# A hybrid attention/RWKV-7/MoE decoder layer: two projection loops with 512-column products, and the wo weight halves split in other places

## What is computed

```
h = RMSNorm(x); z = h @ w_in                       # 2048 -> 5944 columns
y_a = RMSNorm(sparse attention(z))                 # 8 heads, 1024 wide
y_b = RWKV-7 time mixing(z)                        # 16 heads, 1024 wide
x += concat(y_a, y_b) @ w_out                      # 2048 x 2048
x += (softmax(q k^T) v) @ wo                       # q = RMSNorm(x) @ wq; k, v from 256 memory tokens; 4 heads of 512
x += HierMoE(RMSNorm(x))                           # one of 4 groups, 2 of its 8 experts
out = RMSNorm(x)
```

## Time and profile before

| | us |
|---|---|
| median of 3 runs (lowest, highest) | 1764.54 (1761.72, 1767.03) |
| the profiled execution's own time | 1765.84 |
| its span | 1764.1 |
| PE busy | 1687.6 |
| DVE busy | 1011.5 |
| ACT busy | 760.9 |
| mean granted TensorE clock | 0.986 |

### The profile page before, as it was taken

One profiled execution on the slowest core, in us unless ns is written; L12 is line 12 of the kernel. 1 busy time (PEld: TensorE's weight loads), 2 busy tenths in 40 slices (PEclk: granted clock), 3 DMA queues, 4 the chain that ended last, 5 costly groups with the idle time before them and its releaser, 6 DMA issues.

```text
span 1764.1 us, 29546 instructions
## 1 busy us (share of the span) xinstructions
PE 1687.6 (96%) x12488; PEld 1468.0 (83%) x12488; DVE 1011.5 (57%) x1260; ACT 760.9 (43%) x964; POOL 71.6 (4%) x136
## 2 busy tenths in 40 slices
PE   7999999999999999999999999989999999999996
PEld 5887887878878889999999989967887887888784
DVE  1142533424434554445454334388889889889986
ACT  1011210111114544444343333446776766777674
POOL 4001010101100000000000000000000000000000
PEclk9899999999999999999999999999999999999999
DMA  7430613306126444445535326239998996999993
GB/s 211 143 96 2 198 50 123 123 2 198 50 77 213 151 137 144 136 152 192 190 120 182 127 75 195 112 137 356 376 376 328 380 375 249 372 375 349 357 375 150
DMA packets 173745, 350.77 MB, mean 199 GB/s; under 512 B 12915, under 2 KB 145612, under 8 KB 148172
## 3 DMA queue, kind: packets, MB, share of 16 engines
q1 hardware_dynamic: 173644, 349.30, 56.0%
HBM read 347.18 MB, written 2.10 MB: 198 GB/s over the span
## 4 chain that ended last, share of the span: by engine, by line
PE 85%; DVE 10%; ACT 2%; POOL 1%; issue 1%; DMA 1%; SPq 0%; DVEq 0%; ACTq 0%
PE bank L1288 17%; PE bank L771 16%; PE bank L1133 10%; PE bank L1307 9%; PE bank L1137 5%; PE bank L1029 4%; PE bank L1036 3%; DVE split L2172 3%; PE bank L790 2%; PE bank L760 2%; DVE piece L1993 1%; PE bank L876 1%; PE bank L891 1%; PE bank L886 1%; DVE arena_phases L2276 1%; PE bank L1183 1%
## 5 line engine op out<-in xcount | busy, mean ns | idle before, releaser
L2172 DVE TENSOR_TENSOR split<-weights_raw,split 128x2048 fp32r<-128x2048 f32 x192 | 438.7, 2291 | 53.9 <-ACT split L1711 50.7
L1711 ACT CAST split<-weights_raw 128x2048 fp32r<-128x2048 f32 x192 | 367.2, 1914 | 94.5 <-PE bank L1288 48.3
L1288 PE MATMUL bank<-split,gathered_hi 128*128 128x512 f32 x1024 | 320.6, 394 | 7.0 <-DVE split L2172 6.9
L771 PE MATMUL bank<-arena_fixed 128*128 128x256 f32 x1280 | 302.6, 388 | 0.0
L771 PEld LDWEIGHTS bank<-arena_fixed 128*128 128x128 f32 x1280 | 238.5, 191 | 42.8 <-issue 9.1
L1288 PEld LDWEIGHTS bank<-split,gathered_hi 128*128 128x128 f32 x1024 | 190.2, 189 | 48.1 <-DVE split L2172 9.5
L1288 PE MATMUL bank<-split,gathered_lo 128*128 128x512 f32 x512 | 200.7, 392 | 0.0
L1133 PE MATMUL bank<-loop_split,act_over_concat 128*128 128x256 f32 x768 | 164.8, 283 | 0.0
L1307 PE MATMUL bank<-split,hidden_hi 128*128 128x512 f32 x512 | 161.1, 395 | 1.5 <-DVE hidden_lo L2314 1.0
L2076 DVE TENSOR_TENSOR loop_split<-arena_fixed,loop_split 128x2048 fp32r<-128x2048 f32 x48 | 107.8, 2289 | 90.8 <-ACT loop_split L1608 90.8
L1133 PEld LDWEIGHTS bank<-loop_split,act_over_concat 128*128 128x128 f32 x768 | 129.1, 192 | 0.1
(11 more groups left out here) (396 smaller groups left out, 2388.8 us busy)
## 6 DMA issues: line engine op xcount, KB each, us to landing
weights_raw<-in_moe_w_gate_dram SPq DMA_DIRECT2D x64, 1024.0 KB, 5.0
weights_raw<-in_moe_w_up_dram SPq DMA_DIRECT2D x64, 1024.0 KB, 7.0
weights_raw<-in_moe_w_down_dram SPq DMA_DIRECT2D x32, 2048.0 KB, 7.6
arena_fixed<-in_w_in_dram SPq DMA_DIRECT2D x22, 2048.0 KB, 8.9
arena_fixed<-in_wv_mem_dram SPq DMA_DIRECT2D x8, 2048.0 KB, 8.5
arena_fixed<-in_w_out_dram SPq DMA_DIRECT2D x8, 2048.0 KB, 8.1
arena_fixed<-in_wq_mem_dram SPq DMA_DIRECT2D x8, 2048.0 KB, 8.1
arena_fixed<-in_wo_mem_dram SPq DMA_DIRECT2D x8, 2048.0 KB, 8.3
```

Source lines behind the costliest of these rows:

```text
L771: mm = pe.matmul(b[:, half * T:half * T + T], w[:, c, half * P:half * P + P], hT[:, c, :], start=st, stop=en)
L1288: mm = pe.matmul(bank[parity][:, :], hs[a][:, group % 2, NC // 4 * off + c, :], sl[:, b, c * 2 * FF:(c + 1) * 2 * FF], start=off + c + k == 0,
L1711: nc.scalar.copy(split_half(i, 0, j), raw_half(j, hf, tail)).then_inc(act_hi, 1)
L2172: V.tensor_tensor(split_half(i, 1, j), raw_half(j, hf, tail), split_half(i, 0, j).bitcast(F32), ALU.subtract).then_inc(dve_lo, 1)
```

## The change

It has four parts.

1. For n = 0 and 2 a step takes 512 columns (`WC`) at once. The two slots of a step hold two halves of the rows (8 chunks x 512 columns each) in place of two halves of the columns. A `loop_split` tile is now 4 chunks x 512 columns. PE (`looped_tokens`) does for it 2 token halves x 4 chunks x 3 passes = 24 products of 512 columns, into whole banks, and the pairs of banks alternate from step to step. Row chunks 8 to 15 come first for w_out, in slot 0, so the attention outputs are needed from the third tile on; for wo the outputs of heads 2 and 3 are needed from the third tile on.
2. The residual is added once per step and token half, 128x512; the first token half's add waits for a new semaphore `pe_first`, which PE raises after the last product of that token half, 12 products before the step's end. The squares are 128x512, one per token half, each after its own add, and on ACT they follow the casts. The sums have 4 parts per token half (`SUMMED`).
3. For n = 0 and 2 the loops of PE, DVE and SP are written out, not hardware loops; ACT keeps its loops.
4. The casts and subtractions of wo's second tile pair are moved. ACT: after the copies of heads 2's and 3's probabilities, one half there and one between the output casts of heads 2 and 3. DVE: one half before the lo part of head 2, one between those of heads 2 and 3.

The wq loop keeps its code as `looped_turned`. The core of the diff:

```diff
+        def loop_source(wv_, n, i, s):
+            if n == 1:
+                return wv_[:, :, bass.ds((2 * i + s) * UC, UC)]
+            k = NC // 2 * (s ^ (n == 0))
+            return wv_[:, k:k + NC // 2, bass.ds((2 * i) * UC, WC)]
...
+                if n != 1:
+                    for i in range(1, PAIRS):
+                        for s in range(2):
+                            load_looped(i, s)
+                    continue
...
+            def looped_tokens(n, src, src_ready, turn=0):
+                for q in range(PAIRS):
+                    pe.wait_ge(out_loop, n * NLU + max(2, 2 * q))
+                    for s in range(2):
+                        for h in range(2):
+                            pe.wait_ge(loop_lo, 4 * q + 2 * (NLU * n + s) + h + 1)
+                            pe.wait_ge(src_lo, src_ready[s])
+                            for half in range(2):
+                                b = bank[2 * (q % 2) + half][:, :]
+                                for c in range(NC // 4):
+                                    cc = NC // 2 * (s ^ turn) + NC // 4 * h + c
+                                    for k, (x_, y_) in enumerate(PASSES):
+                                        end = s + h == 2 and c == NC // 4 - 1 and k == 2
+                                        mm = pe.matmul(b, src(x_, cc)[:, half * P:half * P + P],
+                                                       lspl[2 * s + h][:, y_, c * WC:c * WC + WC],
+                                                       start=s + h + c + k == 0, stop=end)
+                                if s + h == 2 and half == 0:
+                                    mm.then_inc(pe_first, 1)
+                        mm.then_inc(pe_loop, 1)
...
-            looped(2, True, normed, (SRC_MEM + MH // 2, SRC_MEM + MH))
+            looped_tokens(2, normed, (SRC_MEM + MH // 2, SRC_MEM + MH))
...
+            def squares(i, n):
                 for tt in range(NT):
+                    act.wait_ge(out_loop, n * NLU + tt + 3 + 2 * i)
+                    A(square_junk[:, tt, bass.ds(i * WC, WC)], x[:, tt, bass.ds(i * WC, WC)], ACT.Square,
+                      accum_out=rms_p[:, tt, bass.ds(i, 1)]).then_inc(squared, 1)
...
-                    if h == 1:
-                        loop_weights(2 * NLU, 1)
+                    if h == MH - 2:
+                        loop_half(1, 1)
+                if (what, h) == ("t", MH - 1):
+                    act.wait_ge(loop_full[1], 16 * NLU + 16)
+                    loop_half(1, 0)
...
+                    if residual and s == 1:
                         for tt in range(NT):
+                            if tt == 0:
+                                dve.wait_ge(pe_first, i + PAIRS * (n // 2) + 1)
+                            else:
+                                dve.wait_ge(pe_loop, 2 * i + n * NLU + 2)
+                            xs = x[:, tt, bass.ds(i * WC, WC)]
+                            V.tensor_tensor(xs, xs, bank[2 * (i % 2) + tt][:, :], ALU.add).then_inc(out_loop, 1)
...
-            loop_weights(2 * NLU, 1)
+            loop_half(2 * NLU, 1, 0)
             output_lo(MH - 2)
+            loop_half(2 * NLU, 1, 1)
             output_lo(MH - 1)
```

More of the change, by code:

```diff
@@ L685, in _ @@
                     sp.dma_start(rb[:, NGR:], router_expert_b[0].partition_broadcast(P)).then_inc(s_late, 16)
-                with sp.Fori(int(n != 1), NLU // 2) as i:
+                if n != 1:
[3 more added lines that the diff above has]
+                    continue
+                with sp.Fori(0, NLU // 2) as i:
                     for s in range(2):
@@ L1128, in looped @@
                                 for c in range(NC // 2):
-                                    cc = NC // 2 * (h ^ turn) + c
                                     for k, (x_, y_) in enumerate(PASSES):
[L1131 to L1138, removed]
+                                        at = c * UC + half * P
+                                        mm = pe.matmul(b, lspl[2 * s + h][:, y_, at:at + P], src(x_, NC // 2 * h + c),
+                                                       start=h + c + k == 0, stop=h == 1 and c == NC // 2 - 1 and k == 2)
                         mm.then_inc(pe_loop, 1)
@@ L1605, in _, with loop_half, loop_weights @@
                     gap2()
[L1606 to L1610, removed]
+            def loop_half(s, h):
+                nc.scalar.copy(lspl[2 * s + h][:, 0, :], slot(s)[:, h * HU:h * HU + HU]).then_inc(loop_hi, 1)
+            def loop_weights(at, s):
                 act.wait_ge(loop_full[s], 8 * at + 16)
                 for h in range(2):
-                    loop_half(s, h, turn)
-            def squares(i, s, n):
-                act.wait_ge(out_loop, n * NLU + s + 3 + 2 * i)
+                    loop_half(s, h)
+            def squares(i, n):
                 for tt in range(NT):
-                    A(square_junk[:, tt, bass.ds((2 * i + s) * UC, UC)], x[:, tt, bass.ds((2 * i + s) * UC, UC)], ACT.Square,
-                      accum_out=rms_p[:, tt, bass.ds(2 * i + s, 1)]).then_inc(squared, 1)
+                    act.wait_ge(out_loop, n * NLU + tt + 3 + 2 * i)
+                    A(square_junk[:, tt, bass.ds(i * WC, WC)], x[:, tt, bass.ds(i * WC, WC)], ACT.Square,
+                      accum_out=rms_p[:, tt, bass.ds(i, 1)]).then_inc(squared, 1)
             def loop_stream(n, out_copy=False, last=False):
                 def step(i, s, weights):
-                    if out_copy:
+                    if out_copy or weights:
                         act.wait_ge(pe_loop, 2 * i + n * NLU + s + 1)
-                    else:
-                        squares(i, s, n)
                     if out_copy:
@@ L1635, in step @@
                     if weights:
-                        loop_weights(2 * i + n * NLU + 2, s, turn)
-                turn = int(n == 0)
+                        loop_weights(2 * i + n * NLU + 2, s)
+                    if not out_copy and s == 1:
+                        squares(i, n)
                 with act.Fori(0, NLU // 2 - 1) as i:
@@ L1652, in _ @@
                 normed_hi("na", f, c_nsa, lambda c: over_hT[:, c, :]).then_inc(src_hi, 1)
-            loop_half(0, 1, 1)
-            loop_weights(0, 1, 1)
+            loop_half(0, 1)
+            loop_weights(0, 1)
             loop_stream(0)
@@ L1819, in rms @@
                     dve.wait_ge(squared, SUMMED[name])
-                    link(V.tensor_reduce(rms_s, rms_p[:, :, 0:4] if name == "nf" else rms_p, AX.X, ALU.add))
+                    link(V.tensor_reduce(rms_s, rms_p if name == "na" else rms_p[:, :, 0:4], AX.X, ALU.add))
                 else:
@@ L2089, in _ @@
                 normed_lo(f, c_nsa, lambda c: over_concat[:, c, :], lambda c: over_hT[:, c, :]).then_inc(src_lo, 1)
-            loop_half(0, 0, 1, 1)
-            loop_weights(0, 1, 1)
+            loop_half(0, 0, 1)
+            loop_weights(0, 1)
             def loop_stream(n, residual=True, last=False):
                 def step(i, s, weights):
-                    if residual:
-                        dve.wait_ge(pe_loop, 2 * i + n * NLU + s + 1)
+                    if residual and s == 1:
                         for tt in range(NT):
-                            xs = x[:, tt, bass.ds((2 * i + s) * UC, UC)]
-                            ins = V.tensor_tensor(xs, xs, bank[2 * s + tt][:, 0:UC], ALU.add)
-                        ins.then_inc(out_loop, 1)
-                    if weights:
-                        loop_weights(2 * i + n * NLU + 2, s, turn)
-                turn = int(n == 0)
+                            if tt == 0:
[4 more added lines that the diff above has]
+                            V.tensor_tensor(xs, xs, bank[2 * (i % 2) + tt][:, :], ALU.add).then_inc(out_loop, 1)
+                    if weights:
+                        loop_weights(2 * i + n * NLU + 2, s)
+                if residual:
+                    for i in range(PAIRS):
+                        for s in range(2):
+                            step(i, s, i < PAIRS - 1 or (s == 0 and not last))
+                    return
                 with dve.Fori(0, NLU // 2 - 1) as i:
```

31 lines of the change are left out of this document (17 added, 14 removed).

## The result

The changed kernel took 1750.16 us (median of 4 runs, 1748.86 to 1752.25) against 1765.63 us (median of 4, 1761.72 to 1767.03) for the one before. The ratio is 0.9917 with a 95% interval of 0.9898 to 0.9937: 14.7 us less, between 11.1 and 18.0. (The medians themselves lie 15.5 us apart.) At a line of 2%, 35 us, it counts as the same; at the 0.3% of the prediction it is faster. A later comparison with 5 runs gave 0.9899 (0.9882 to 0.9915), 1749.69 against 1767.35 us. The forecast was 1748.0 us, 0.9906 of the 1764.54 us that it started from, with a range of 1743.5 to 1755.5.

A forecast was written before the change was run, and what follows sets the result against it. PE was taken as the bound, busy 1687.6 of 1764.1 us. Terms of 9.9, 6.1 and 0.5 us sum to 16.5, giving 1748.0 us from the median of 1764.5; range 1743.5 to 1755.5 us.

The forecast's parts named there:

- rival d: Loops' ends: the clock holds there too, up to 3.2 us more at one loop, 1744.8 us; chance 0.12.
- Term 1: w_out and wo loops: 384 products of 512 columns at 226.7 ns each replace 768 at 120.0; 9.9 us less.
- The wait at the start of w_out: Start of w_out: PE still waits for DVE's tile 1, so the first tile's 0.3 us gain becomes a wait.
- Term 2: Memory heads: head 2's values start 3.5 us sooner and the clock holds, 2.6 us more; 6.1 us less.
- Term 3: Ends of both loops: sums start some 1.5 us after the last product, not 1.75; 0.5 us less for both.
- (a): Heads: clock falls before head 2's values anyway, or DVE or ACT hold them longer; gain 3.5 us, 1750.6 us; chance 0.08.
- (b): Both loops: 512-column products cost 232.9 ns as at L1307; gain 5.5 in place of 10.2 us, 1752.7 us; chance 0.12.
- (c): Both loops: 512-column products cost 240 ns, so widening gains nothing; 1757.9 us; chance 0.03.
- (e): Both loops: fetching written-out code makes PE wait, up to 49 us, time 1797; chance 0.03.
- The third unit of wo: wo loop: this tightest load is in time, needed 21.8 us after the start, with 2.6 us of slack; costs nothing.

The follow-up runs named there:

- gap filled: Kernel before, with 17 unused products on PE after the memory heads' last transposes: 1763.09 us, ratio 0.9978.
- written out: Kernel before, with only PE's loops over w_out and wo written out in place of the hardware loop: ratio 1.0004.
- part 4 alone: Kernel before, with only wo's second tile pair's casts and subtractions moved behind the probability copies: 1758.97 us, ratio 0.996.
- other banks: Changed kernel, with head 2's outputs in PSUM banks 2 and 3 and head 3's in 5 and 6: 1748.52 us, ratio 0.9901.
- changed, again: The changed kernel itself, unaltered, measured again in a later comparison with the kernel before: 1749.69 us, ratio 0.9899.
- all but part 4: Changed kernel, with wo's weight casts put back before the probability copies: 1755.3 us, ratio 0.9938.
- alternate banks: Changed kernel, with the wide products changing PSUM bank after every three, not every twelve: 1750.39 us, ratio 0.9905.
- late adds: Changed kernel, with both token halves' adds waiting for the end of the step: 1750.73 us, ratio 0.9909.
- busy ends: Changed kernel, with 11 idle products on PE at the end of the w_out and wo loops: 1746.74 us, ratio 0.9885.
- busy ends, other banks: Changed kernel, with idle products at both loops' ends and swapped PSUM banks for heads 2 and 3's outputs: 1746.33 us, ratio 0.9882.

## Why the prediction was right, and where it was not

The sum was 16.5 us, and the profiled span is shorter by 15.6 us (1764.1 to 1748.5). Step by step:

| step | forecast | measured in the chain |
|---|---|---|
| w_out loop | -4.8 | -4.7 (first product to last: 807.45 to 900.12, 809.17 to 897.13) |
| wo loop | -5.1 | -5.1 |
| heads | -6.1 | -5.4 |
| sums after the loops | -0.5 | -0.5 |
| clock behind the loops' ends | 0 (rival d: up to -3.2 at one) | -1.3 and -1.5 |
| before the w_out loop | 0 | +1.7 |
| after the norm before the MoE | 0 | +1.2 |

The total lies so near the forecast partly by luck. The three costed terms gave 15.7 us in place of 16.5; the clock behind the loops' ends, put at nothing, gave 2.8 more, and 2.9 were lost in two places that the change does not touch. Those two are scatter between executions. The first product of w_out stands at 807.45, 808.04, 811.10 and 811.37 us in the profiles of four kernels whose code up to there is the same (before, gap filled, written out, part 4 alone). From the MoE's first gate product to the end, the twelve profiles take 592.9 to 594.5 us; from the last product of wo to that gate product, the 32 transposing instructions left out, those four kernels take 28.6 to 29.8 us.

**Term 1** held to a tenth: 226.8 against 226.7 ns. The wait at the start of w_out came as costed:

```profile
815.17 0.30 PEld L1149 LDWEIGHTS bank<-loop_split,rwkv_outputs_hi 128*128 128x128 f32 x2 [0.71 <-DVE loop_split L2108]
```

The weight load waits 0.71 us for tile 1, where it waited 0.22 before. The reason I gave for 226.7 rather than 232.9 ns (the bank change) fell with the experiment. So the choice of L1288's price was right, but its reason was not, and what does set the two prices apart is not shown. L1288's own groups of 24 do not all cost 226.7 ns either: 21 of the 55 in the chain of before do, 27 cost 228.8 to 229.2. At 229 ns each loop would have gained 0.9 us less. The Trainium skill's figure (TensorE: Matmul & The Clock Gate, "Wait — 56ns, not 53.3ns?") of about 2.5 ns beside the columns does not fit products that each carry a weight load: here it was 13.3 to 13.5 ns, and merging two saved 13.2.

**Term 2** is the one that was off: 6.1 forecast, 5.4 measured. The mechanism was right in both its halves: the clock gave 2.7 us (2.6 forecast), and the shorter wait 2.7 (3.5 forecast). The step that failed is "PE's values of head 2 start 3.5 us sooner, at about 1030.1, after 0.9 us of idle time". I had checked ACT's order and not all of PE's waits at that instruction. `memory_values` also waits for DVE's lo part of head 1, since head 2's outputs go into head 1's banks. Under the 4.4 us of before that wait had been over for 2.8 us when PE started and had no row of its own. Its end was in the trace of before all the same:

```profile
1029.49 1.29 DVE L2126 TENSOR_TENSOR act_over_hT<-bank,act_over_concat 128x512 fp32r<-128x512 f32 x2 [2.76 <-ACT act_over_concat L1678]
```

It ends at 1029.49 + 1.29 = 1030.8, 0.7 us behind my start. The run with other banks took this wait away, and the idle time fell to 0.78 us.

**Term 3** came out at 1.5 us from last product to sum (897.1 to 898.62), as summed:

```profile
898.62 0.16 DVE L1852 TENSOR_REDUCE arena_fixed<-arena_fixed 128x2 f32<-128x8 f32 x1 [0.79 <-ACT square_junk L1651]
```

**Rivals.** (a) came true in part: the clock held behind 1.70 us, but DVE did hold head 2's values, by 0.8 of the 2.6 us that (a) put at stake. (b) and (c) are out by the chain, (e) by the written-out kernel. (d) was half seen. I had treated the clock there as decided by the length of the idle time, and it is not. The clock fell at both ends in the changed kernel's profile, at a cost 1.3 and 1.5 us lower than before; in its second profile it did not fall at all behind the wo loop. The row of before for that place:

```profile
1138.85 6.73 PE L790 MATMUL bank<-norm_diagonals,arena_phases 128*128 128x128 f32 x32 [3.22 <-DVE norm_diagonals L1831]
```

The 1.5 us there can't be credited to the change: the kernel with part 4 alone has the old loop and the same 3.22 us of idle, and its 32 instructions take 5.47 us. (d)'s price was also too high: at the full rate the 64 transposing instructions take 7.81 us, not 7.1, so 2.5 us were to be had and not 3.2.

The third unit of wo landed in time: ACT sat idle for 10.75 us before it and cast at 1046.89, 13.7 us after PE's first product of wo.

By their ratios the two comparisons measured 14.7 and 17.9 us less, one on each side of the sum.

## What to carry to other kernels

When a long wait is taken away, list every wait of the instruction behind it, on every engine, with the time at which each was over. The next one to end sets the new start, and the old trace does not name it as a wait. Wide products pay for the time that one product costs beside its columns: take that price from products of the same form in the same kernel. A wait of TensorE can cost twice, once itself and once in the half-rate clock behind it (at the heads, the shorter wait and the clock were worth 2.7 us each), so it pays to look at the granted clock after each idle time of some microseconds. When a total meets its forecast, add up the steps all the same: errors can cancel, as 2.8 and 2.9 us did here.

## What the runs showed of the hardware

- With PE's idle time filled by products that compute nothing, the clock held: 7.81 and 3.84 us for transposes that took 9.04 and 5.23, and 7.17 for values that took 9.89. Taking the wait away is not needed for that part of the gain.
- The same idle time can cost or not, and a longer one can cost less. This is what all twelve profiles show behind the w_out and the wo loop (idle time of PE, then the time of the transposing instructions; at the full rate they take 7.81 and 3.84 us):

| profile | w_out: idle, then 64 take | wo: idle, then 32 take |
|---|---|---|
| before | 3.15, 10.34 | 3.22, 6.73 |
| before, written out | 3.14, 10.13 | 3.21, 6.68 |
| part 4 alone | 3.15, 10.12 | 3.22, 5.47 |
| before, gap at the heads filled | 3.14, 7.81 | 3.21, 5.47 |
| changed | 2.89, 9.04 | 2.96, 5.23 |
| changed, again | 2.89, 9.15 | 2.95, 3.84 |
| all but part 4 | 2.89, 9.16 | 2.96, 5.47 |
| other banks | 2.88, 9.16 | 2.96, 5.38 |
| alternate banks | 2.89, 9.04 | 2.96, 5.23 |
| late adds | 3.50, 9.28 | 3.56, 5.46 |
| busy ends | 0.43, 7.81 | 0.51, 3.84 |
| busy ends, other banks | 0.43, 7.81 | 0.50, 3.84 |

What decides it within this range stays open. Behind the shorter idle times looked at here, 0.58, 0.78 and 1.70 us at the heads and 1.94 us, the clock was whole; behind 4.37 us it fell.

- The price of a 512-column product did not depend on how often its PSUM bank changed between two banks: 226.8 ns either way.
